# Fetching u and v as one 8 KB row for three of four token tiles, and one to one for the first

## The reference

```python
def block(t):                                   # t: tokens x 1024
    q = (t @ wq).reshape(PEER_BLOCK, PEER_HEADS, 2, PEER_DQ // 2)
    s1 = jnp.einsum('thd,nd->thn', q[:, :, 0], k1)
    s2 = jnp.einsum('thd,nd->thn', q[:, :, 1], k2)
    v1, i1 = lax.top_k(s1, PEER_TOPK)
    v2, i2 = lax.top_k(s2, PEER_TOPK)
    ...
    score, ci = lax.top_k(cand, PEER_TOPK)
    expert = i1[ci // 16] * PEER_NKEYS + i2[ci % 16]
    g = jax.nn.softmax(score, axis=-1)
    act = jax.nn.gelu(jnp.einsum('thkd,td->thk', u_tab[expert], t))
    return jnp.einsum('thk,thkd->td', g * act, v_tab[expert])
```

## Time and profile before

| what | value |
|---|---|
| median of 3 runs | 4290.01 us (4275.37 to 4290.02) |
| span of the profiled execution | 4287.8 us |
| busy: PE, DVE, POOL, ACT | 3534.2, 2141.1, 1437.5, 910.5 us |
| moved by DMA in all | 765.15 MB |
| first and last fetch of the peer layer issued at | 2519.3 and 4244.2 us |

### The profile page before, as it was taken

The page is one execution under the profiler, slowest core; times in us unless marked ns, Lnnn a source line. Parts: engine busy times, 40 slices in busy tenths (PEclk is TensorE's granted clock), DMA queues, the critical chain, the costliest instruction groups (busy, mean ns, idle before and its releaser), DMA issues.

```text
span 4287.8 us, 33127 instructions
## 1 busy us (share of the span) xinstructions
PE 3534.2 (82%) x10814; PEld 1820.1 (42%) x10814; DVE 2141.1 (50%) x4648; ACT 910.5 (21%) x1890; POOL 1437.5 (34%) x1337
## 2 busy tenths in 40 slices
PE   8377999999997999979999875678777777777776
PEld 4244544444453564456544563234333333333232
DVE  0557234421013567746344458764678776334432
ACT  1234411000032225622110322111122212111111
POOL 0214400000000006400000023354777776777774
PEclk9668999999999989979899987889898898988998
DMA  3010111333211113201212456675998999999996
GB/s 153 8 50 1 57 62 69 157 149 129 95 59 54 59 54 106 81 35 62 101 39 98 154 188 224 236 281 200 375 350 324 353 369 334 366 371 363 369 360 244
DMA packets 171912, 765.15 MB, mean 178 GB/s; under 512 B 19256, under 2 KB 19256, under 8 KB 160224
## 3 DMA queue, kind: packets, MB, share of 16 engines
q0 software_dynamic: 157904, 580.06, 36.8%
q1 hardware_dynamic: 13824, 182.97, 11.4%
q10 hardware_dynamic: 16, 0.02, 0.0%
HBM read 744.08 MB, written 18.89 MB: 178 GB/s over the span
## 4 chain that ended last, share of the span: by engine, by line
PE 50%; DVE 18%; issue 10%; POOL 5%; DMA 3%; ACT 3%; another core or an unknown queue 2%; POOLq 0%; DVEq 0%; ACTq 0%
PE ps L252 14%; PE ps L258 11%; DVE arena L2782 7%; PE ps L1416 6%; PE ps L1346 5%; POOL arena L2752 4%; PE ps L2705 4%; PE ps L1722 2%; PE ps L220 2%; DMA arena<-in_pu,arena 1%; DMA arena<-in_pv,arena 1%; PE ps L1709 1%; DVE arena L2613 1%; DVE arena L2619 1%
## 5 line engine op out<-in xcount | busy, mean ns | idle before, releaser
L2705 PE MATMUL ps<-arena 128*128 128x512 f32 x2048 | 1029.6, 658 | 395.5 <-issue 195.0
L2705 PEld LDWEIGHTS ps<-arena 128*128 128x128 f32 x2048 | 411.3, 208 | 991.1 <-issue 881.0
L2782 DVE CUSTOM_DVE_ANT_0 arena<-arena 128x1024 f32<-128x1024 f32 x512 | 622.6, 1221 | 367.3 <-DMA arena<-in_pu,arena 337.6
L252 PE MATMUL ps<-arena 128*128 128x512 f32 (+1 forms) x1768 | 755.9, 588 | 32.0 <-ACT arena L2271 24.4
L2752 POOL DMA_INDIRECT arena<-in_pu,arena x512 | 547.7, 1070 | 422.7 <-issue 98.1
L2752 POOL DMA_INDIRECT arena<-in_pv,arena x512 | 563.1, 1100 | 204.3 <-issue 127.1
L258 PE MATMUL ps<-arena 128*128 128x512 f32 (+2 forms) x1408 | 529.5, 537 | 3.1 <-DVE arena L1263 0.9
L252 PEld LDWEIGHTS ps<-arena 128*128 128x128 f32 x1768 | 337.9, 192 | 435.7 <-issue 430.6
L258 PEld LDWEIGHTS ps<-arena 128*128 128x128 f32 x1408 | 267.6, 191 | 262.0 <-issue 216.8
L220 PE MATMUL ps<-arena 128*128 128x128 f32 x1046 | 194.5, 321 | 206.0 <-ACT arena L812 49.8
L2721 ACT ACTIVATE arena<-arena 128x128 f32<-128x128 f32 x512 | 192.8, 397 | 751.1 <-PE ps L2705 360.6
(11 more groups left out here) (342 smaller groups left out, 3399.5 us busy)
## 6 DMA issues: line engine op xcount, KB each, us to landing
arena<-in_w_in SPq DMA_DIRECT2D x27, 2048.0 KB, 8.9
arena<-in_w_ada SPq DMA_DIRECT2D x12, 2048.0 KB, 8.0
arena<-in_w_ff_in SPq DMA_DIRECT2D x8, 2048.0 KB, 12.5
arena<-in_w_ff_out SPq DMA_DIRECT2D x8, 2048.0 KB, 12.5
arena<-in_w_pq SPq DMA_DIRECT2D x8, 2048.0 KB, 8.5
aside<-arena POOLq DMA_DIRECT2D x20, 512.0 KB, 4.5
arena<-in_w_at SPq DMA_DIRECT2D x4, 2048.0 KB, 8.9
arena<-in_w_o SPq DMA_DIRECT2D x4, 2048.0 KB, 8.7
```

The costliest lines, as they stand in the source:

```text
L252: x = t.matmul(PS[:, b, 0:n], hT[:, k, i * 128:(i + 1) * 128], w[:, k, :], start=k == 0, stop=k == nk - 1)
L2705: x = t.matmul(PS[:, b + c, :], DG[n % 4], row(f)[:, 512 * c:512 * c + 512], start=j == 0, stop=j == 127)
L2782: v.tensor_tensor_reduce(row(f), row(f), TT[i], 1.0, 0.0, ALU.mult, ALU.add, DOT[i % 2][:, j:j + 1]).then_inc(*pe.V.step("dot", 128 * i + j))
```

## The change

- Tables u and v become one table `uv`, a row of u and the row of v of the same expert side by side (8 KB).
- Tiles 1 to 3: one fetch of 128 rows of 8 KB (1 MB) brings u and v of a choice. There are 384 of them, into 14 places of 8 KB (PAIRS), used in turn. Five of those share memory with places of tile 0 and first wait for them. A place is free when the add of its choice is done.
- Tile 0: 256 fetches of 4 KB half rows (the table seen as 32768 half rows), u by index 2e and v by 2e+1. DVE doubles an index list and writes a second one (one more small instruction for each of 8 heads). They use 7 places all the way.
- The list of work rows (now WORK) is, for tile 0: u alone for 32 choices, then u and v in turn with v 32 behind, then 32 v. For tiles 1 to 3: u and v in turn, v LAG = 10 choices behind.
- Blocks of the gelu are 8 choices in tiles 1 to 3 (16 in tile 0), and the cubic takes 2 DVE operations in place of 3 (of the 5 in a block, 4 remain). Two late steps of each tile move from v choice 96 and 100 to 112 and 116, and the buffers YY and XHR move by 4 KB.

```diff
-        BL = 16
-        FETCH = []
+        BLOCK = (16, 8, 8, 8)
+        LAG = 10
+        WORK = []
         done_v = 0
-        for n_ in range(1, 513):
-            FETCH.append(("pu", (n_ - 1) // 128, (n_ - 1) % 128))
-            goal = 0 if n_ < 64 else (n_ - 64) // 4 if n_ < 128 else 16 + (n_ - 128) * 5 // 4 if n_ < 512 else 512
-            while done_v < goal:
-                FETCH.append(("pv", done_v // 128, done_v % 128))
+        for n_ in range(1, 129):
+            WORK.append(("pu", 0, n_ - 1))
+            while done_v < n_ - 32:
+                WORK.append(("pv", 0, done_v))
                 done_v += 1
+        WORK += [("pv", 0, j_) for j_ in range(done_v, 128)]
+        for n_ in range(384 + LAG):
+            if n_ < 384:
+                WORK.append(("pu", 1 + n_ // 128, n_ % 128))
+            if n_ >= LAG:
+                WORK.append(("pv", 1 + (n_ - LAG) // 128, (n_ - LAG) % 128))
...
-        PLACES += [panel("w_pq+", c)[:, 1024 * j:1024 * j + 1024] for c in (1, 2, 3) for j in range(4)]
+        PAIRS = [panel("w_pq+", c)[:, 2048 * j:2048 * j + 2048] for c in (1, 2, 3) for j in range(2)]
+        PAIRS += [piece(o, 2048) for o in (o_va + 1024, o_ka + 2048, o_qa + 2048, o_ka, o_cs, W0, o_t + 2048, o_ht)]
...
+                    g.indirect_dma_start(CELLS[k], None, HALVES, bass.IndirectOffsetOnAxis(ap=x, axis=0)).then_inc(s_row_in[k], 16)
+                else:
+                    g.wait_ge(*pe.V.at("sel", i, j // 16))
+                    g.indirect_dma_start(PAIRS[k - FEW], None, UV, bass.IndirectOffsetOnAxis(ap=EXU[i][:, j:j + 1], axis=0)
+                                         ).then_inc(s_row_in[k], 16)
```

More of the change, by code:

```diff
@@ new lines, in build @@
+        PAIRS += [piece(o, 2048) for o in (o_va + 1024, o_ka + 2048, o_qa + 2048, o_ka, o_cs, W0, o_t + 2048, o_ht)]
+        MANY = len(PAIRS)
+        SHARED = {7: (2,), 9: (6, 1), 10: (3, 0), 11: (4,), 13: (5,)}
+        FETCH = [f for f in WORK if f[1] == 0]
+        SPOT = [n % FEW for n in range(256)]
+        FETCH += [("uv",) + f[1:] for f in WORK if f[1] and f[0] == "pu"]
+        SPOT += [FEW + n % MANY for n in range(384)]
+        FETCHES = len(FETCH)
+        NTH, PREV, uses, held_by = [], [], [0] * (FEW + MANY), [None] * (FEW + MANY)
@@ new lines, in build, with number, emptied @@
+        for n_ in range(FETCHES):
+            k_ = SPOT[n_]
+            PREV.append([held_by[k_]] if uses[k_] else [held_by[c] for c in SHARED.get(k_ - FEW, ())])
+            uses[k_] += 1
+            NTH.append(uses[k_])
+            held_by[k_] = FETCH[n_]
+        NUMBER = {f: n for n, f in enumerate(FETCH)}
+        s_row_in = [sem(f"s_in{j}") for j in range(FEW + MANY)]
+        def number(f):
+            return NUMBER[f if f[1] == 0 else ("uv",) + f[1:]]
+        def emptied(f):
+            return ("pu" if f[0] == "pu" else "pv",) + f[1:]
@@ L2526, in fetched @@
+        FREED = [max((WHEN[emptied(f)] for f in before), default=-1) for before in PREV]
         def fetched(f):
-            return s_row_in[SPOT[NUMBER[f]]], 16 * NTH[NUMBER[f]]
+            return s_row_in[SPOT[number(f)]], 16 * NTH[number(f)]
         def row(f):
-            return PLACES[SPOT[NUMBER[f]]]
+            n = number(f)
+            if f[1] == 0:
+                return CELLS[SPOT[n]]
+            o = 1024 * (f[0] == "pv")
+            return PAIRS[SPOT[n] - FEW][:, o:o + 1024]
@@ L2683, in in_order @@
             for r in range(ROWS):
-                while n < ROWS and PREV[n] < r:
+                while n < FETCHES and FREED[n] < r:
                     tab, i, j = FETCH[n]
-                    while tab == "pu" and (i, j // 16) not in ready:
+                    while tab != "pv" and (i, j // 16) not in ready:
                         advance(r)
@@ L2732, in gather @@
                 tab, i, j = FETCH[n]
-                if PREV[n] >= 0:
-                    tab0, i0, j0 = FETCH[PREV[n]]
+                k = SPOT[n]
+                for tab0, i0, j0 in PREV[n]:
                     if tab0 == "pu":
@@ L2797, in rows_vector @@
                     v.tensor_scalar(LATE[3], LATE[3], ALPHA, None, ALU.mult).then_inc(*pe.V.step())
-                if f and tab == "pv" and j == 100:
+                if f and tab == "pv" and j == 116:
                     v.wait_ge(s_xhr, 16 * (i + 1))
```

105 lines of the change are left out of this document (58 added, 47 removed).

## The result

| kernel | median of runs (us) | ratio to the kernel before (95% interval) |
|---|---|---|
| before | 4290.02 | 1 |
| changed | 4348.57 (4343.81 to 4354.03) | 1.0145 (1.0120 to 1.0169) |

A forecast was written before the change was run, and what follows sets the result against it. The prediction took POOL's issuing of 4 KB fetches beside DVE's dots to hold DMA back after some 3000 us. Its terms, 3115 + 3 + 456 + 590 + 8 + 38, gave 4210 us of span, 4212 as a run; range 4132 to 4280.

The forecast's parts named there:

- Part 1: Tile 0 up to the first 1 MB fetch: 3115 us as before, plus and minus between -35 and +35 us.
- rival on tile 0: Tile 0 gets slower, as 47 more adds come at a low PE clock: +67 us, 4279 us; chance 0.08.
- The price of a fetch: Tiles 1 to 3: a 1 MB fetch of 8 KB rows takes 2.54 us at 413 GB/s, at most 2.89.
- bytes rival: Memory gives random rows only 363 GB/s, so 2.89 us a choice in tiles 1 to 3: 4276 us; chance 0.12.
- split rival: POOL splits each 8 KB row in two pieces, so the old cadence stays: about 4290 us; chance 0.05.
- Part 2: Tiles 1 to 3 while selection runs: DVE sets the pace, 163 choices at 2.80 us, 456 us.
- the ring: Tiles 1 to 3: a fetch waits until a place comes free behind a block's gelu; priced within 2.80 and 2.67 us a choice.
- Part 3: The 221 choices left after selection: 2.67 us each, the middle of 2.56 to 2.78, 590 us.
- way round: From a block's last landing through gelu, add and new fetch to its dot: 10.4 or 12.1 us by PE's clock.
- 8 us that I had put on top: Ends of tiles 1 and 2: POOL stands behind DVE at the layer norm, some 4 us each.
- The ring decides: Rival: a longer loop in tiles 1 to 3, up to 4271 or 4357 us; break-even 2.93 us a choice; chance 0.09.
- What would show it: Signs in the profile: POOL waiting for PE 1 or 2 us a block if right, several us if the ring decides.

The follow-up runs named there:

- t0cells: lag8 with 8 more 4 KB places for tile 0 from its fetch 192 on; 4196.3 us beside 4193.7 for the kernel before.
- t0mix: lag8 with the first six u choices of tile 1 among tile 0's last v choices; 4182.6 us beside 4193.7 for the kernel before.
- lag8: The changed kernel with LAG 8 in place of 10; 4195.4 us beside 4293.5 for the kernel before.
- blk4: The changed kernel with blocks of 4 in tiles 1 to 3 and LAG 4; 4194.7 us beside 4293.5 for the kernel before.
- lag12: The changed kernel with LAG 12 in place of 10; 4663.6 us beside 4293.5 for the kernel before.
- lag9: The changed kernel with LAG 9 in place of 10; 4259.8 us beside 4193.7 for the kernel before.
- mix8: t0mix run again unchanged, on another chip; 4181.2 us beside 4193.3 for the kernel before.
- again: The kernel before, unchanged, profiled and timed beside itself on chip 7; 4291.4 us beside 4293.6.
- lag8b: lag8 run again unchanged on chip 7; 4193.5 us beside 4293.6 for the kernel before.
- again3: The kernel before, unchanged, profiled and timed beside itself on chip 15; 4198.6 us beside 4193.4.

## Why the prediction was wrong

**Part 1, 3115, measured 3142.6.** Both bounds were 35 us, so it is inside them. The new adds found the room that I gave them: from 2600 to 2850 us PE is busy 186 of 250 us at a clock of 0.91, where it was 145 at 0.78. So the rival on tile 0 did not come about. I said that the 7 places are no tighter than before up to row 144, and did not price what comes after it: there were 19 before, and the changed kernel keeps 7. From 3000 to 3095 us DMA moves 326 GB/s where before it was 386 from 3000 to 3100, and PE waits for rows. From 3095 on 32 adds stand behind each other at 1.72 us with PE 53.9 of 55 us busy. Eight more places alone gave nothing in t0cells, so what the places cost by themselves is not shown; that the last v can be overlapped is (t0mix, 12 to 14 us).

**The price of a fetch: 2.54 us, measured 2.49** (the median distance of two dots in lag8 and blk4; where 2.48 stands, it is the same figure, within 0.01). The bytes rival (363 GB/s) is wrong by lag8's 415. The split rival, POOL making two pieces of a row, is wrong too: a 1 MB fetch holds POOL for 0.94 us, as one of 512 KB did.

**Part 2, 459 us with the first landing, measured 508.** Two terms failed. The first dot comes 20.3 us after the first fetch, where I had 3 beyond its share: it isn't the landing that it waits for, but tile 0's 32 late adds and its layer norm, which stand ahead of it on DVE. The distance is 20.3 us in each of ten profiles with this tile 0, whatever the lag. That is 17 us. The other is the pitch: 2.99 us for 2.80, 31 us. With the ring open it is 2.68 (lag8), with DVE busy 385 of the 437 us from 3163 to 3600, so DVE's pace of 2.74 was near. The ring, which I gave 0.06 us a choice, costs 0.31.

**Part 3 is the step that failed, by the price that it puts on the ring: 2.67, measured 2.99.** The mechanism stood in the prediction, and the way round that it gave for the low clock, 12.1 us, is what was measured: 12.1 in the block shown, 12.4 in the mean. That is no luck of terms that cancel: from the dot to the issue of the freed fetch I had 6.45 us and it is 6.3, from there to its dot 5.63 and it is 5.64 in the median. What was mis-sized is what a block costs once the way is longer than the cover. A block was forecast at 21.4 us, and takes 23.9:

| | forecast | measured | difference |
|---|---|---|---|
| block's end to the dot of the freed fetch | 11.2 (the middle of 10.4 and 12.1) | 12.4 | +1.2 |
| the four choices behind it | 4 x 2.54 = 10.2 | 3.29 + 3.00 + 2.72 + 2.55 = 11.6 | +1.4 |

The first line is mostly my choice of the middle: I took PE's clock as low in part of the first adds, and it is low in each block (0.50 from 1 to 5 us behind the block's last dot, in the mean of 25 blocks). The second has no term in the sum at all: I let the late fetch be followed at DMA's full rate. After DMA has run dry the next two 1 MB fetches take 3.3 and 3.0 us (3.4 and 3.1 in lag12, over the same 25 blocks), and that comes back in each block. 2.6 us in each of 27.6 blocks is 71 us, and 590 + 71 = 661, where 658 was measured. The means hold the end of a tile, so nothing is left for the 8 us that I had put on top for two of them. All these differences, 28 + 17 + 31 + 60 - 1 = 135, are the distance from 4210 to 4345.

Set against lag8, the whole price of the ring can be read: I gave it 0.06 us a choice in part 2 and 0.13 in part 3, 39 us in all. It costs 2.99 - 2.68 = 0.31 in the one and 2.99 - 2.54 = 0.45 in the other, 150 us; the medians differ by 153. Lag8's 4195 us with 39 on top would still have been faster than 4290; with 153 it is not.

**The rivals.** "The ring decides" was the one that held. It got 0.09, and asked for a way round of 13.3 us at break-even and 13.8 for slower (the run's 2.2 us over the span was added there where it had to be taken off: 2.98 us a choice and 13.6); the kernel is slower with 12.4, by the tail behind it. Its break-even in the pitch, 2.93 us a choice, stands: the changed kernel is over it with 2.99 and slower than 4290, lag9 under it with 2.83 and 2.72 and at 4260.

**What would show it.** I said POOL would wait several us for PE in each block if the ring decides. It does (9.28 in the block above). But lag8's POOL waits 5 to 7 us in each block too, since it issues eight fetches in a burst, and loses nothing. The sign that told them apart is at the other end: gaps of DVE for DMA that are longer than in the steady pace (3.41 and 2.51 for 1.25), and 213 GB/s in a stretch of 3 us.

The balance by lag, due time against a way round of 12.1 to 12.4 us: LAG 8 14.9 us, LAG 9 12.4, LAG 10 9.9, LAG 12 5.0. LAG 9 is just even, and measured near halfway (4260 between 4195 and 4349). My prediction had 10.2 against 10.4 or 12.1, short or even at best, and put a small price on it.

## What the change is worth with the ring open

lag8 is the same change with one number different (blk4 with two): 4195 us, 2.3% less than before on chips where before takes 4290. On chips where before takes 4194 lag8 itself wasn't run; its variants t0cells, t0mix and mix8 take 4196, 4183 and 4181 there, equal to before or 0.3% under it. So I take what the change gains to lie in that 4 KB fetches run at 355 to 363 GB/s on some chips, and 8 KB ones at 415 there. On chip 7, where both were profiled, it is 355 (again) against 415 (lag8b) from 3600 to 4140 us; on a chip where before is fast t0cells moves 416 and the kernel before, on another such chip, 394 (again3). That this difference of rates is all of the gain is not shown.
